# Three blocks on one core: six feature buffers that begin 32 to 192 bytes behind a multiple of 512 bytes

## What is computed

```python
# first block
out = merged @ w_out                                     # 256 x 2048 by 2048 x 2048
# second block
hid = silu(einsum("bsd,df->bsf", x, w_gate)) * einsum("bsd,df->bsf", x, w_up)   # f = 5632
ffn = einsum("bsf,fd->bsd", hid, w_down)
ple = sigmoid(einsum("bsd,de->bse", x, w_ple_gate)) * einsum("bsq,qd->bsd", p, w_ple)
x = layer_norm(ALPHA * x + ffn + ple, ln2_g, ln2_b)
```

## Time and profile before

| what | value |
| --- | --- |
| median of two runs | 3394.03 us |
| span of the profiled execution, first to last instruction | 3388.4 us |
| between the two | 5.6 us |
| TensorE matmul busy | 3255.3 us, 96% |
| VectorE busy | 2275.4 us, 67% |
| ScalarE busy | 1517.0 us, 45% |
| mean granted clock of TensorE | 0.990 of 2.4 GHz |

### The profile page before, as it was taken

The page is one execution under the profiler, slowest core; times in us unless marked ns, Lnnn a source line. Parts: engine busy times, 40 slices in busy tenths (PEclk is TensorE's granted clock), DMA queues, the critical chain, the costliest instruction groups (busy, mean ns, idle before and its releaser), DMA issues.

```text
span 3388.4 us, 71888 instructions
## 1 busy us (share of the span) xinstructions
PE 3255.3 (96%) x30322; PEld 3103.4 (92%) x30322; DVE 2275.4 (67%) x2978; ACT 1517.0 (45%) x1835; POOL 74.3 (2%) x154
## 2 busy tenths in 40 slices
PE   8999899999998999999999999999989999999998
PEld 8998888888898769999999999989879899999998
DVE  8776856565687977777655544565656777777545
ACT  5442454443244035544444343453454555545443
POOL 0000100000000000000000000000000000000000
PEclk9999999999999999999999999999999999999999
DMA  8758723232786544677655555534424455555554
GB/s 322 261 204 329 273 86 107 86 108 92 279 346 238 187 161 175 252 290 283 240 190 194 193 195 198 187 127 165 159 100 163 162 191 192 186 187 193 190 197 152
DMA packets 94146, 664.19 MB, mean 196 GB/s; under 512 B 10353, under 2 KB 10993, under 8 KB 15346
## 3 DMA queue, kind: packets, MB, share of 16 engines
q1 hardware_dynamic: 74736, 540.05, 44.4%
q0 software_dynamic: 14400, 104.86, 8.0%
q10 hardware_dynamic: 4802, 16.12, 1.2%
HBM read 654.70 MB, written 6.29 MB: 195 GB/s over the span
## 4 chain that ended last, share of the span: by engine, by line
PE 86%; DVE 9%; ACT 2%; issue 1%; DMA 1%; ACTq 0%; SPq 0%; DVEq 0%
PE ps L463 22%; PE ps L462 22%; PE ps L464 21%; PE ps L434 4%; PE ps L657 4%; PE ps L641 2%; PE ps L493 2%; PE ps L642 2%; PE ps L643 2%; DVE ring_parts L1837 2%; DVE work L1860 1%; DVE work L2113 1%; PE ps L506 1%; DVE ring_parts L1845 1%; PE ps L650 1%
## 5 line engine op out<-in xcount | busy, mean ns | idle before, releaser
L1837 DVE TENSOR_TENSOR ring_parts<-ring,ring_hi 128x1024 fp32r<-128x1024 f32 x866 | 1042.1, 1223 | 701.2 <-ACT ring_hi L1158 687.3
L1158 ACT ACTIVATE ring_hi<-ring 128x1024 fp32r<-128x1024 f32 x866 | 909.4, 1059 | 1141.6 <-PE ps L464 1094.9
L463 PE MATMUL ps<-h_lo,ring_hi 128*128 128x256 f32 x2624 | 729.2, 278 | 0.0
L462 PE MATMUL ps<-h_hi,ring_hi 128*128 128x256 f32 x2112 | 593.1, 281 | 15.8 <-DVE h_lo L1867 8.5
L464 PE MATMUL ps<-h_hi,ring_parts 128*128 128x256 f32 x2112 | 585.1, 277 | 0.0
L463 PEld LDWEIGHTS ps<-h_lo,ring_hi 128*128 128x128 f32 x2624 | 497.7, 190 | 1.4 <-issue 1.2
L462 PE MATMUL ps<-x_hi,ring_hi 128*128 128x256 f32 x1664 | 466.3, 280 | 9.7 <-DVE x_lo L1867 5.8
L463 PE MATMUL ps<-x_lo,ring_hi 128*128 128x256 f32 x1664 | 462.9, 278 | 0.0
L464 PE MATMUL ps<-x_hi,ring_parts 128*128 128x256 f32 x1664 | 461.0, 277 | 0.0
L462 PEld LDWEIGHTS ps<-h_hi,ring_hi 128*128 128x128 f32 x2112 | 397.0, 188 | 18.2 <-issue 9.8
L464 PEld LDWEIGHTS ps<-h_hi,ring_parts 128*128 128x128 f32 x2112 | 397.0, 188 | 0.0
(11 more groups left out here) (471 smaller groups left out, 5781.3 us busy)
## 6 DMA issues: line engine op xcount, KB each, us to landing
ring<-in_weights SPq DMA_DIRECT2D x511, 1024.0 KB, 4.8
work<-in_ada POOLq DMA_DIRECT2D x96, 1024.0 KB, 6.7
work<-in_c_row POOLq DMA_DIRECT2D x4, 1024.0 KB, 5.6
gate_store<-gate_out ACTq DMA_DIRECT2D x8, 512.0 KB, 6.2
work<-gate_store ACTq DMA_DIRECT2D x2, 2048.0 KB, 19.4
resid<-in_lora ACTq DMA_DIRECT2D x9, 256.0 KB, 5.4
resid<-in_x SPq DMA_DIRECT2D x4, 512.0 KB, 6.0
resid<-in_x ACTq DMA_DIRECT2D x1, 2048.0 KB, 28.0
```

The lines of the kernel that those rows point to most:

```text
L462: mm(o, w_hi[:, k, cols], hi(kc), start=(kc == 0 and m % 2 == 0), stop=False, skip_group_check=True)
L463: mm(o, w_hi[:, k, cols], lo(kc), start=False, stop=False, skip_group_check=True)
L1158: A(high_ring(n)[:, 2 * (e % 2) + half, :], ring[:, n % RING, half * (SLOT // 2):(half + 1) * (SLOT // 2)], ACT.Copy)\
L1837: tt(lo, x, high_ring(n)[:, e % 4, :].bitcast(F32), ALU.subtract).then_inc(S("lo_ready"), 1)
```

## The change

Numbers in `own` and `w` are words of four bytes. `M1_HI` moves by 16 words, `HID_LO` by 8, `X_HI` by 16, `X_LO` by 24, `HID3_LO` by 32, `H3_HI` by 48. What lies behind them in the work area makes room: `GU`, `GU2`, `GU3`, `P2`, `P2_HI`, `P2_LO` and `MOD4` move by 32 words, `UP3` and `UC` by 64. No instruction, loop, wait or transfer is added or taken away.

```diff
--- before.py
+++ after.py
@@ -291,9 +291,9 @@
     HI_Z2 = own("ring_hi2", 27184, 2, SLOT // 2)
     G_OUT = nc.alloc_sbuf_tensor_at("gate_out", [P, 4 * T], F32, offset=red_at)[:]
     ZR_HI, ZR_LO = own("zr_hi", 26624, 8, T), own("zr_lo", 12288, 8, T)
-    M1_HI, M1_LO = own("m1_hi", 14336, DC, T), own("m1_lo", 0, DC, T)
+    M1_HI, M1_LO = own("m1_hi", 14352, DC, T), own("m1_lo", 0, DC, T)
     SHB = w(31296, 2, 4, T)
-    MOD4 = w(34816, FFN2_COLUMNS)
+    MOD4 = w(34848, FFN2_COLUMNS)
     NKK = X[:, 0:8, :]
     TW = X[:, 8:12, :]
     SG1 = X[:, 12:16, :]
@@ -336,10 +336,10 @@
     SGB, TB, TB2 = w(18688, 4, T), w(19712, 4, T), w(12544, 4, T)
     PRE = w(12544, DC, T)
     MIX_HI, MIX_LO = own("mix_hi", 22528, DC, T), own("mix_lo", 4352, DC, T)
-    HID_HI, HID_LO = own("hid_hi", 0, 44, T), own("hid_lo", 11264, 44, T)
-    X_HI, X_LO = own("x_hi", 22528, DC, T), own("x_lo", 26624, DC, T)
-    GU, GU2, GU3 = w(30720, 4, T), w(31744, 4, T), own("gu", 32768, 4, T, dt=F32)
-    P2, P2_HI, P2_LO = w(33792, 2, T), own("p_hi", 34304, 2, T), own("p_lo", 33792, 2, T)
+    HID_HI, HID_LO = own("hid_hi", 0, 44, T), own("hid_lo", 11272, 44, T)
+    X_HI, X_LO = own("x_hi", 22544, DC, T), own("x_lo", 26648, DC, T)
+    GU, GU2, GU3 = w(30752, 4, T), w(31776, 4, T), own("gu", 32800, 4, T, dt=F32)
+    P2, P2_HI, P2_LO = w(33824, 2, T), own("p_hi", 34336, 2, T), own("p_lo", 33824, 2, T)
     BROW = w(20736, 2 * COLS)
     HI = own("ring_hi", 35504, 4, SLOT // 2)
 
@@ -360,10 +360,10 @@
     SQL = w(26624, DC, T)
     NORM3 = w(4096, DC, T)
     HS_HI = own("hs_hi", 21568, DC, T)
-    HID3_HI, HID3_LO = own("hid3_hi", 4096, FF3_CHUNKS, T), own("hid3_lo", 15360, FF3_CHUNKS, T)
-    H3_HI, H3_LO = own("h3_hi", 26624, DC, T), own("h3_lo", 0, DC, T)
-    UP3 = w(30720, 8, T + 2)
-    UC = own("uc", 32784, 8, T, dt=F32)
+    HID3_HI, HID3_LO = own("hid3_hi", 4096, FF3_CHUNKS, T), own("hid3_lo", 15392, FF3_CHUNKS, T)
+    H3_HI, H3_LO = own("h3_hi", 26672, DC, T), own("h3_lo", 0, DC, T)
+    UP3 = w(30784, 8, T + 2)
+    UC = own("uc", 32848, 8, T, dt=F32)
     GSIG = UP3[:, 0:4, 2:T + 2]
     SQF, OUT = w(0, DC, T), w(26624, DC, T)
```

## The result

The changed kernel took 3431.25 and 3432.18 us, median 3431.72, against 3394.03 before: a ratio of 1.0109 with a 95% interval of 1.0085 to 1.0134. It is slower by 1.1%, which lies inside the 2% band, on the other side of no change from the forecast of 3367 us and outside its range of 3340 to 3421.

A forecast was written before the change was run, and what follows sets the result against it. The prediction took TensorE's matmul pace as the bound: 4064 threes at 6.7 ns less each give 27.1 us, so the span falls from 3388.4 to 3361.3 us; 5.6 us from span to run gives 3367 us, range 3340 to 3421.

The forecast's parts named there:

- What bounds the kernel: Whole kernel: the pace of TensorE's matmuls is the time, TensorE busy for 96% of the 3388.4 us span.
- The notch: Threes of matmuls: two steady rhythms, 346.7 and 353.3 ns, lie 6.7 ns apart; 31.7 us over 4752 threes.
- the far bound of 324 ns: A three with nothing in the way, estimated from plain float32 matmuls: 22.7 ns below the present 346.7.
- (a): Output projection w_out: m1_hi moves by 64 bytes, m1_lo stays; 256 threes, each forecast 6.7 ns faster.
- (e): Second feed-forward: h3_hi at 192 bytes, h3_lo at 0; 1408 threes, each forecast 6.7 ns faster.
- the next notch down: Price taken for 4064 threes in the shifted stages: 340 ns instead of 346.7, 27.1 us less; chance 0.40.
- (c): First feed-forward's down projection: hid_hi at 0, hid_lo at 32 bytes; 704 threes, each forecast 6.7 ns faster.
- a notch up: Rival, chance 0.22: shifted stages settle at 353.3 ns a three, 27.1 us more over 4064 threes, 3421 us.
- (b): First feed-forward and its gate: x_hi at 64 bytes, x_lo at 96; 1664 threes, each forecast 6.7 ns faster.
- (f): Second feed-forward's down projection: hid3_hi at 0, hid3_lo at 128 bytes; 688 threes, priced at nothing.
- (d): Small p buffers: p_hi and p_lo both at 128 bytes; 32 threes, called too small to matter.
- Nothing happens: Rival, chance 0.25: the rhythm stays at 346.7 ns a three whatever the placement, 3394 us.

The follow-up runs named there:

- 511 combinations: Threes alone, other engines idle, rounded feature at 0, places of the remainder and both weights varied: two at 340.0 ns, median 353.4, slowest 373.
- 416 random sets: Threes alone, other engines idle, with the places of all four operands drawn at random: none fell below 340.0 ns a three.
- the sweep: Threes alone, other engines idle, over 256 pairs of feature places, weights at 192 and 128 bytes: 346.6 ns at 0, 0; 356.6 at 64, 96.

## Why the prediction was wrong

**What bounds the kernel: right.** TensorE's pace in the threes is the time of the stages touched, no wait and no other engine came in there, and the addresses reach into the pace. VectorE's and ScalarE's busy times did not move.

**The notch: right as a size.** Many paces stand on 340.0, 346.7, 353.3 and 360.0, others lie between or above them. The 340 ns below that no row had shown exists; the far bound of 324 ns does not, in 511 combinations and 416 random sets.

**The step that failed** is the price of (a) to (e): of two ends, 353.3 above and a notch below, it took the one below, "the next notch down", though the only rows of another pace, 353.3 and 357.5, lay above. The reason given was that the loss is "in the phase between streams" and movable. It is, but movable says nothing of the sign. The step took the places before for an ordinary draw, from which a shift could as well gain. They were no such draw: with weights at 192 and 128 bytes, 0, 0 is the minimum of the features' map, and only three of its 64 cells, 0, 0 and 0, 128 and 0, 224, have 346.6. With these weights a shift of the features could lose or keep, not gain. The gain of a notch lay with the weights, which the change left alone. Instead of -27.1 us the four stages gave +32.5.

**Term by term.** (a), (c) and (e) went one notch up, with the rival "a notch up", whose price of 27.1 us over 4064 threes fits them. That (e) was no worse is chance: the sweep has 360.0 as well as 353.3 for its places. (b) was mis-sized by it too: 10.0 ns a three, one and a half notches, a rhythm that closes over six threes only (365, 354, 356, 353, 356 and 356 ns in the trace); that alone adds 5.5 us. (f), priced at nothing from w_out3, came out at 0.0 us: 256 is as good as 0, and 0, 128 is one of the three good cells. Some luck is in that, for w_out3 itself, in the same cell, ran a notch higher in the same execution. (d), 32 threes, is too small to matter. The part in untouched stages had no term at all, and the range ended at 3421, one notch up: with the 5.5 us of (b) and the 5.2 us that the medians leave outside the four stages the time lies 11 us beyond. The 5.6 us that the sum adds from the span to the time are a difference between two executions; within one it is 1.3 us.

**The rivals.** "A notch up" came true, with a chance of 0.22. "Nothing happens" had two sights for it, and the rule of the Trainium skill, "TensorE: Matmul & The Clock Gate", part 2, step 1: two independent SBUF read ports, one for the streaming operand and one for the weight load. No run here bears out that placement is therefore free: with the same instructions and idle engines the sweep's threes took 346.6 to 366.7 ns by the features' places, and 340.0 with other places of the weights. The measurement decides; what in the machine makes it so is not shown.

**What stays open.** Why the distances count modulo 256 bytes, and which of the pairs meet, was not found: no single distance orders the map. Why zr, the convolution's input projection, w_out3 and some cells of the sweeps have two rhythms at the same distances, and what makes a stage keep one of them, is open as well.

## What to carry to other kernels

When back-to-back matmuls are the bound, map their pace over the places of all operands, stationary ones too, in a small program of the matmuls alone; its numbers came back in w_out, ffn2, down2 and down3 of this kernel to within 0.3 ns, except where a place has two rhythms. A placement that looks arbitrary may be the best of its row: to know that the pace can change does not say which way. Move what stands in the same relation to all stages (here three weight buffers and the ring) before moving the buffers of each stage.

## What the runs showed of the hardware

A three of float32r matmuls, 128 x 128 by 128 x 256, took 340.0 to 373 ns by the distances of its operands modulo 256 bytes, often a multiple of 6.67 ns, 16 periods of 2.4 GHz, apart. At its best all three starts lie 113.3 ns apart. Shifting all operands together changed no pace by more than 0.9 ns. The same places can hold two paces: w_out3 of the changed kernel ran at 346.7 ns up to its 32nd three and then at 353.3. And in the kernel with the weights moved, a pause of 4.1 us of TensorE was followed by 8 us at a mean granted clock of 0.67, so that the stage, 1.7 us shorter by its threes, came out 4.7 us longer: 6.4 us for a pause of 4.1.
